# Two-block transformer step on one core: the mixer of the second block rewoven, with its small products between the input chunks, both z chunks ahead of the delta rule's pairs, and idle products around the norms

## The reference

```python
x = layer_norm(ALPHA * x + swiglu_half(x, ffn1...), ln1...)
h = x @ w_in
a_u, a_v, b_qkv, b_z, b_beta, b_decay, c_q, c_k, c_v, c_r, c_g = split(h)
out_a = spatial_gating(gelu(a_u), gelu(a_v), ...)        # per 128 tokens, 4 heads
out_b = gated_deltanet(b_qkv, b_z, b_beta, b_decay, ...)  # 8 heads, chunks of 64 tokens
out_c = gla(c_q, c_k, c_v, c_r, c_g, ...)                 # 4 heads, chunks of 64 tokens
mix = concatenate([out_a, out_b, out_c]) @ w_out
x = layer_norm(ALPHA * x + mix, ln2...)
x = layer_norm(ALPHA * x + swiglu_half(x, ffn2...), ln3...)
```

## Time and profile before

| | |
|---|---|
| median of 3 runs | 3182.92 us (3181.77 to 3183.39) |
| the profiled execution | 3187.82 us |
| its span, first to last instruction | 3185.7 us |
| TensorE busy | 2966.3 us (93%) |
| VectorE busy | 1318.6 us (41%) |
| ScalarE busy | 1110.5 us (35%) |
| GpSimd busy | 818.0 us (26%) |
| DMA | 257.50 MB, mean 81 GB/s |
| mean granted TensorE clock | 0.961 |

### The profile page before, as it was taken

How to read it: one execution, slowest core, us unless ns; L and a number is a source line. 1 busy time by engine, 2 the same in 40 slices (tenths; PEclk the granted TensorE clock), 3 DMA queues, 4 the chain that set the end, 5 groups by cost and what they waited for, 6 DMA issues and landing times.

```text
span 3185.7 us, 46789 instructions
## 1 busy us (share of the span) xinstructions
PE 2966.3 (93%) x19136; PEld 2399.5 (75%) x19136; DVE 1318.6 (41%) x1507; ACT 1110.5 (35%) x1290; POOL 818.0 (26%) x288
## 2 busy tenths in 40 slices
PE   7999999889999999988799999999999978899997
PEld 5776677658788887768678888788877858678886
DVE  3534444343223235636552323422157454643215
ACT  4334434422233325532233323333236421233323
POOL 4112211230101263334001135011443432000144
PEclk9999999979999999989999999999999989899998
DMA  4111111112222332210022233222332200122233
GB/s 167 40 60 53 43 45 46 53 53 93 94 92 92 111 140 88 93 54 1 15 79 93 92 119 135 81 104 92 125 126 84 84 28 1 41 80 95 103 125 113
DMA packets 36094, 257.50 MB, mean 81 GB/s; under 512 B 4032, under 2 KB 4080, under 8 KB 5872
## 3 DMA queue, kind: packets, MB, share of 16 engines
q1 hardware_dynamic: 34416, 249.65, 21.7%
q0 software_dynamic: 1536, 5.83, 0.6%
HBM read 253.30 MB, written 2.16 MB: 80 GB/s over the span
## 4 chain that ended last, share of the span: by engine, by line
PE 72%; issue 12%; DVE 6%; POOL 5%; ACT 3%; DMA 0%; ACTq 0%; DVEq 0%; POOLq 0%; SPq 0%
PE ps L2056 42%; PE ps L1572 6%; PE ps L1527 5%; PE ps L1564 4%; POOL wl L1194 4%; PE ps L2169 3%; PE ps L1627 2%; PE ps L1616 2%; PE ps L885 1%; ACT wh L1771 1%; PE ps L1582 1%; DVE wl L1882 1%; PE ps L1657 1%; DVE sqa L1915 1%; PE ps L2135 1%
## 5 line engine op out<-in xcount | busy, mean ns | idle before, releaser
L1194 POOL TENSOR_TENSOR wl<-raw,wh 128x2048 fp32r<-128x2048 f32 x114 | 525.2, 4607 | 817.7 <-ACT wh L1771 817.7
L2056 PE MATMUL ps<-xh,wh 128*128 128x512 f32 x1680 | 664.0, 395 | 20.7 <-DVE qkv L648 11.0
L2056 PE MATMUL ps<-xl,wh 128*128 128x512 f32 x1680 | 658.2, 392 | 0.0
L2056 PE MATMUL ps<-xh,wl 128*128 128x512 f32 x1680 | 658.0, 392 | 0.0
L1771 ACT ACTIVATE wh<-raw 128x2048 fp32r<-128x2048 f32 x224 | 427.5, 1908 | 408.1 <-PE ps L2056 351.9
L1882 DVE TENSOR_TENSOR wl<-raw,wh 128x2048 fp32r<-128x2048 f32 x112 | 285.7, 2551 | 578.8 <-ACT wh L1771 557.0
L2056 PEld LDWEIGHTS ps<-xh,wh 128*128 128x128 f32 x1680 | 317.7, 189 | 92.6 <-issue 14.7
L2056 PEld LDWEIGHTS ps<-xl,wh 128*128 128x128 f32 x1680 | 318.0, 189 | 67.8 <-issue 2.4
L2056 PEld LDWEIGHTS ps<-xh,wl 128*128 128x128 f32 x1680 | 317.8, 189 | 66.7
L1736 POOL TENSOR_TENSOR hl<-hf,hh 128x1024 f32 x44 | 105.8, 2404 | 980.8 <-ACT hh L1781 980.8
L2056 PE MATMUL ps<-hh,wh 128*128 128x512 f32 x704 | 277.1, 394 | 1.6 <-POOL wl L1194 1.2
(11 more groups left out here) (361 smaller groups left out, 4663.1 us busy)
## 6 DMA issues: line engine op xcount, KB each, us to landing
raw<-stream SPq DMA_DIRECT2D x232, 1024.0 KB, 4.8
btw<-bias_rows POOLq DMA_DIRECT2D x2, 1536.0 KB, 8.9
x<-x_in SPq DMA_DIRECT2D x1, 2048.0 KB, 8.2
out<-x SPq DMA_DIRECT2D x4, 512.0 KB, 2.6
sgp<-sg POOLq DMA_DIRECT2D x2, 640.0 KB, 4.0
cst<-consts SPq DMA_DIRECT2D x1, 1092.0 KB, 12.2
c<-bias_consts SPq DMA_DIRECT2D x1, 1024.0 KB, 15.7
bt<-bias_rows POOLq DMA_DIRECT2D x2, 512.0 KB, 9.2
```

Source lines behind the costliest of these rows:

```text
L1194: nc.gpsimd.tensor_tensor(wl[:, p, :], raw[:, p, :], wh[:, p, :].bitcast(F32), ALU.subtract).then_inc(s["chunk_lo"], 1)
L2056: mm = te.matmul(dst, wslice(w, k), r(k), start=(start and m == 0), stop=(stop and m == len(steps) - 1))
```

## The change

Input chunks come in another order (cqk, au, rows, cv, av, cr, six of q, k, v, then z). All chunks from cr on are cut in four quarters (`chunk_q`), and `between` puts a small group after a quarter: linear attention, spatial product, decay columns, head norms. The head norm is by token: `norm_columns` has mean squares as columns, the root and reciprocal are 16 wide, `norm_spread` spreads the result over a tile's features in PSUM. Both z chunks run whole ahead of pair 0. All pairs use banks 4 to 7; values and keys by token are made pair by pair among the pairs. The factor steps go to GpSimd, three behind each of the first four levels' masks. w and u are copied per pair. The output product goes by half tiles over k tiles 0, 1, 6, 7 first (branches done early) and 2 to 5 after. `busy(n)` issues n products of 128 columns whose result nobody reads. Buffers are moved to make room (addresses only).

```diff
-        IN_ROWS, IN_CQK, IN_CV, IN_AU, IN_AV, IN_CR, IN_Z = range(6, 13)
+        IN_CQK, IN_AU, IN_ROWS, IN_CV, IN_AV, IN_CR, IN_QKV, IN_Z = 0, 1, 2, 3, 4, 5, 6, 12
+        def norm_columns(l, pe, g, tiles, bank, src):
+            for t in range(tiles):
+                pe.wait_ge(s["head_square"], l * NORMED + 2 * g + t + 1)
+                for m in range(4):
+                    c = 16 * g + 8 * t + 2 * m
+                    mm = nc.tensor.matmul(ps[:, bank, c:c + 2], tmp[:, src + t, m * P:(m + 1) * P], head_mean2, start=True, stop=True)
+            mm.then_inc(s["head_ms"], 1)
+        def norm_spread(l, pe, g, t, bank):
+            pe.wait_ge(s["head_rstd"], l * GROUPS + g + 1)
+            for m in range(4):
+                for b in range(2):
+                    c = 16 * g + 8 * t + 2 * m + b
+                    mm = nc.tensor.matmul(ps[64 * b:64 * b + 64, bank, m * P:(m + 1) * P], ncol[:, 1, c:c + 1].to_broadcast([P, 64]), C("ident"), start=True, stop=True)
+            mm.then_inc(s["head_spread"], 1)
...
+        def between(l, pe, j, q):
+            g = j - 8
+            at = (j, q)
...
+            if 0 <= g < 4 and q == 1:
+                norm_columns(l, pe, g, 2, 5, 4)
...
+            if at in ((10, 2), (10, 3)):
+                pe.wait_ge(*((s["gla_dve"], l * 16 + 16) if q == 2 else (s["gla_half"], l * 2 + 2)))
...
+            if at == (11, 2):
+                norm_columns(l, pe, 4, 2, 5, 4)
+            if 0 <= g < 4 and q in (3, 4):
+                t = q - 3
+                if g or t:
+                    pe.wait_ge(s["head_normed"], l * NORMED + 2 * g + t)
+                norm_spread(l, pe, g, t, 4)
...
+            for j in (IN_Z, IN_Z + 1):
+                for t in range(2):
+                    z_tile(j, t)
+            pair(0)
+            pair(1)
+            pe.wait_ge(evac[1], n_evac(l, 1, OFF_IN) + IN_Z // 2 + 1)
+            turned(0)
+            pair(2)
+            pe.wait_ge(evac[0], n_evac(l, 0, OFF_IN) + IN_Z // 2 + 1)
+            turned(1)
...
-            dve.wait_ge(s["wu_ps"], l * 2 + 2)
-            ve.tensor_copy(u_own[:, :, :, :], ps[:, 4:8, :].rearrange("p a (c t) -> p a c t", t=CH)).then_inc(s["wu_sb"], 1)
+            for pr in range(PAIRS):
+                dve.wait_ge(s["wu_ps"], l * 8 + 4 + pr + 1)
+                ve.tensor_copy(u_own[:, pr, :, :], chunks(ps[:, 4 + pr, :])).then_inc(s["u_sb"], 1)
...
+            def busy(n):
+                for _ in range(n):
+                    te.matmul(shift_ps[:, 0:P], C("ident"), C("feat_mean"), start=True, stop=True)
             def norm(l, w):
...
+                busy(12)
...
+                for n in (0, 1):
+                    out_half(n)
+                norm_columns(l, pe, 5, 4, 2, 1)
+                out_half(2)
+                for pr in range(PAIRS):
+                    if pr:
+                        pe.wait_ge(s["head_normed"], l * NORMED + 10 + pr)
+                    norm_spread(l, pe, 5, pr, 1)
+                    out_half(3 + pr // 2, (0, 1) if pr % 2 == 0 else (2, 3))
...
+                out_half(11, (0, 1))
+                shift(l, 1)
+                out_half(11, (2, 3))
+                for n in (12, 13, 14):
+                    out_half(n)
+                out_half(15, (0, 1))
+                sums(l, 1)
+                out_half(15, (2, 3))
+                busy(4)
```

More of the change, by code:

```diff
@@ L233 @@
     "ln_square_sum": "added to the sum of squares",
-    "out_early": "the last but one tile of the mixer's product is in PSUM",
-    "out_early_x": "and added to x",
+    "out_tile": "tiles 2 and 3, then 4 and 5, then 6 of the mixer's product are in PSUM",
+    "out_early_x": "tile 4, then tile 6 is added to x",
     "ln_mean": "mean of the shifted tiles, over all partitions",
@@ L250 @@
     "head_square": "squares of a tile",
-    "head_ms": "each head's mean square",
+    "head_ms": "mean squares of a group of tiles, by token",
     "head_std": "root",
     "head_rstd": "reciprocal",
+    "head_spread": "a tile's reciprocals over its features",
     "head_normed": "normed tile",
@@ L258 @@
     "gla_gate_act": "ScalarE: steps of the gates",
+    "gla_half": "TensorE: scores, then outputs of the first two heads",
     "gla_keys": "keys by token",
@@ L274 @@
     "mixed_lo": "and its lo part",
-    "by_token_ps": "keys, then values by token in PSUM",
+    "by_token_ps": "a pair's values, then keys by token in PSUM",
     "by_token_sb": "and in SBUF",
@@ L333 @@
     "factor_act": "exponentials of the factors by token",
-    "factor_dve": "keys and values times factors",
+    "factor_dve": "factors ahead of their exponentials, beta exp(gamma)",
+    "factored": "keys and values of a pair times factors (GpSimd)",
     "level_x": "X = (L masked) T in PSUM",
@@ L340 @@
     "level_l": "masked L",
-    "wu_ps": "-(T beta k exp(gamma))^T, then T beta v in PSUM",
-    "wu_sb": "and in SBUF",
+    "wu_ps": "a pair's -(T beta k exp(gamma))^T, then T beta v in PSUM",
+    "w_sb": "the former in SBUF (ScalarE)",
+    "u_sb": "the latter in SBUF (VectorE)",
     "rec_state": "the state before a chunk",
@@ L994, in mixer_pool @@
             gp = nc.gpsimd
-            for j in range(IN_CR + 1):
+            for j in range(IN_Z):
                 rest(pool, c_no(l, OFF_IN) + j + 2, j % 2)
@@ L2252, in down_chunks, with out_chunks @@
     return pad(b)
+def out_chunks(w):
+    b = w.reshape(KT, P, KT, P)
+    return np.stack([np.concatenate([b[k, :, t] for h, t in OUT_HALVES[4 * m:4 * m + 4] for k in OUT_K[h]], 1) for m in range(OUTP)])
 def layer_chunks(a, l):
```

766 lines of the change are left out of this document (431 added, 335 removed).

## The result

The changed kernel takes 3149.36 us (median of 4 runs, 3144.4 to 3150.43), the kernel before beside it 3183.15: a ratio of 0.989, 95% interval 0.9873 to 0.9907. It is faster, by 34 us and not by the 63 of the forecast, and lies 3 us above the range. The profiled execution has a span of 3147.9 us against 3185.7, so its stretches have to account for 37.8.

The account below looks back on a forecast made before the run. TensorE's work plus its gaps was taken to bound the kernel. Terms of -28.1 us a layer, twice, and three starts made -62.8: profiled 3187.82 to 3125, median of runs 3182.92 to 3120 us; range 3098 to 3146.

Parts of the forecast that it names:

- Input products: Input stretch of a layer, with small groups now among the chunks: 185.5 us against 176.50, +9.0.
- a return: Input stretch: each of 21 switches from a small group back to long products costs 0.25 us, 5.2 in all.
- Rival C: Input chunks 8 to 13: small groups drop the clock, chunks 9.6 us dearer each, 3235 us; chance 0.04.
- The gap: Between last z chunk and first pair: nothing left except one wait, -31.8 us a layer.
- Pairs: From the pairs to the second level's first product: 7.0 us a pair, 49.9 against 47.80, +2.1 a layer.
- Rival A: Pairs and first level become the bound: low clock, a pair 9 us, eight to eleven us a layer, 3140; chance 0.12.
- Start of the recurrence: TensorE's 2.72 us wait for one copy becomes four copies that run with the products, -2.4 us a layer.
- Output product: Mixer's output product by half tiles, finished branches first: 61.8 us against 66.80, -5.0 a layer.
- Its steps are the same: Output product behind the shift: VectorE's steps unchanged, 16.8 us from first product to the sums over squares.
- 3.2 to the end: Output product, its remaining part at the end: 3.2 us within the 61.8.
- Idle products: Around the norms: twelve small products in the wait bring the clock back, -2.2 us a start, three starts beyond the input term.
- rival B: Idle products around norms run at the low clock and delay starts, +1.9 us each, 3140 us; chance 0.10.

Follow-up runs that it names:

- the last kernel: Changed kernel with pair waits filled, lo parts earlier, no idle products at the boundary, columns later and split, idle products around the sums: 3110.14 us, ratio 0.9754.

## Why the prediction was wrong

The direction and the mechanism were right: the gap of 31.8 us went wholly in both layers, and its work fitted where the forecast put it. The step that failed is the price of the products behind a wait, nearly all of which were taken at the high level; most of all the pairs' "(1.05 and 0.98 us)", which took 2.07 and 1.97 in the second pair.

- *Input products*, +9.0: the sum was right but for one term. Without the wait in chunk 11 the stretch is 183.9 us, and the forecast's sum without it 185.5 - 1.9 = 183.6. The wait for ScalarE's squares was foreseen at 1.9 (no row stood behind its 10.3 and 8.4 us); it is 1.46, with 2.0 at the low level behind it. The other part of the miss is layer 1, which in the kernel before took 174.8 and not 176.5. A norm group took 3.8 us for 3.9, and a piece of twelve products among the groups starts the next thing 2.85 to 2.95 us later where 2.74 is usual, so 0.1 to 0.2 a return for the 0.25 taken: 1 to 3 us too many over the 21. The first two chunks took 23.5 us for the 21.9 in the sum and made up for it, so that it fits within 0.3 is partly luck. Rival C did not come: the clock is 0.99.
- *The gap*, -31.8: right.
- *Pairs*, +2.1: this is the step that failed most. "Products of pair n+1 (1.05 and 0.98 us)" held for the first pair, for none of the second in layer 0, and for some of the third and fourth. With the clock kept up the period is 7.3 to 7.8 for the forecast 7.0 and the levels begin at 38.6 for 37.3; as the kernel is, 43.0 and 42.2. The levels' start behind LT was right (7.3 for 7.5), though the mask in it came at 5.8. The first level, 12.6, took 13.5 and 13.1. Against the 49.9 of the sum the stretches are 56.5 and 55.3; the table shows layer 1 milder, since there the kernel before took 51.3 and not 47.8. Rival A had named just this (clock down among the small products, 4 us instead of 2, a pair 9) and got 0.12; against it I had set the long z products right ahead, which kept the clock up for the first pair and did nothing for the wait behind it. Its second reason, GpSimd held up, is small: its T step beside VectorE's two gating steps took 1.64 us instead of 1.26, once a layer. The Trainium skill (TensorE: Matmul & The Clock Gate, A second HAM failure mode: psum-queue depth-cycling) tells of a kernel in which short idle times between groups of matmuls on cycling banks let the clock swing; the traces here agree, with 1.50 us of wait and 0.79 of granted clock, and it should have been weighed beside rival A.
- *Start of the recurrence*, -2.4: the 2.72 us wait is gone as forecast. In layer 0 a stop of 1.34 us that the timeline gives to "issue" stands in the last level instead, and 1.0 is left; why TensorE got no instructions there was not tried.
- *Output product*, -5.0: up to the shift 40.0 in layer 0 (forecast 40.7), the wait ahead of the sums 4.74 (4). Two terms fell short. "Its steps are the same" was wrong of VectorE: from the first product behind the shift to the sums over squares are 18.3 us for the 16.8, since VectorE now stands 1.48 us for a half tile among them. The clock has no part in this: from the shift to the first sum are 15.2 us in the kernel before and 16.7 in every one of the other traces, the last kernel's too. The "3.2 to the end" was 4.6: the second sum, 1.87, and the last half tile ran at the low level and were priced at the high one. In layer 1 another 3.2 fell behind the sixteen column products. The runs with the clock held show these last two.
- *Idle products*, -2.2 a start: the price is right where the wait is VectorE's (1.6 and 2.2 in the first two chunks of the inputs, 1.6 and 2.5 behind the mixers), and the sign is wrong at the boundary, +2.8, where I counted a start like the others from a row of another norm. The forecast's bound of +1.9 (rival B) comes near that one place, by another road: rival B had the idle products run at the low level, and there, in the changed kernel's trace, they ran at the high one, 2.84 us for all twelve.

## What to carry to other kernels

Where one engine bounds the kernel and its clock falls at short waits, as here, price a short wait twice: the wait, and all that runs at half speed behind it. Here a wait of 1.46 us cost 3.4 in all, and filling one of 1.03 gave 4.6 to 4.9. A bound that is read in one phase of the trace at the high level holds for the next phase only if no wait lies between; fill the wait first with work from the neighbouring phase, and only what is left with idle products. And price a step in every place where it occurs: the twelve idle products were worth about 2 us at four norms and cost 3 at the fifth.

## What the runs showed of the hardware

- TensorE's granted clock fell at waits of 1.50 us (pairs), 1.46 (chunk 11) and 1.03 (between the sums), each time with small products around it, but not at the same place. In layer 0's pairs the products right behind the wait took 2.07 us, in layer 1's the first of them still 1.12 and the third 2.07; in chunk 11 the columns and six long products went by before the spacing rose from 0.23 to 0.43 us; the second sum was at the low level at once (1.86). Idle products of 128 columns in the waits kept the clock at 1.00 in the pairs and behind the shift of the last kernel; in its input the wait itself is gone.
- How long it stays down after the same wait differs: the twelve long products behind the wait in chunk 11 took 4.2 to 4.6 us in the 18 inputs of nine traces, and 5.31 and 5.47 in the one kernel without idle products, though those had stood 150 us earlier.
- So one program has several fixed times for the same stretch (40.0, 41.6 or 43.2 us to the shift; about 33 or 35 behind it). That is most of what separates two executions of the changed kernel, 3141.9 and 3147.9 us of span, and an edit worth 3 us cannot be read from one stretch in one trace.
- At the boundary between the layers, the time from the start of the last run of 33 long products to the next chunk was 19.6 to 19.9 us in the five traces without idle products there (the kernel before among them) and 22.6 to 23.4 in the nine with them, however fast the norm's own products ran. The profile names VectorE's lo part or "issue" for the wait. Only there the program jumps back in the loop over the layers; that the jump is the cause is an argument, and no run of it was made.
